# GpSimd's bias tables wait for VectorE's qk or low part, and five dot products move from mixer C to mixer B, in a two-layer hybrid encoder

## What is computed

```python
mod = jax.nn.silu(c) @ w_ada + b_ada                     # one row per token group
shift, scale, gate = jnp.split(mod, 3, axis=-1)
h = rms_norm(x, ln_g) * (1.0 + scale) + shift
qa, ka, va = ...   # mixer A: 4 heads, differential attention
qb, kb, vb = ...   # mixer B: 8 heads of 64, neighbourhood attention on a (rows x 64) grid
qc, kc, vc = ...   # mixer C: 12 heads of 128, three dilated windows
s = einsum(qr, kr) * scale + bias                        # B: bias from rpb_b, by relative position
s = jnp.where(col_ok, s, NEG); p = softmax(s)
merged = sum(sigmoid(g_i) * ((y_i * silu(z_i)) @ w_br[i]) for i in A, B, C)
x = x + gate * (merged @ w_out)
```

## Time and profile before

| | us |
|---|---|
| median of three runs | 2292.37 (2291.51 to 2294.75) |
| the profiled execution, device time | 2290.99 |
| its span, first to last instruction | 2289.2 |
| VectorE busy | 1716.5 (75%) |
| ScalarE busy | 1117.2 (49%) |
| GpSimd busy | 59.6 (3%), 103 instructions |

### The profile page before, as it was taken

One profiled execution on the slowest core, in us unless ns is written; L12 is line 12 of the kernel. 1 busy time (PEld: TensorE's weight loads), 2 busy tenths in 40 slices (PEclk: granted clock), 3 DMA queues, 4 the chain that ended last, 5 costly groups with the idle time before them and its releaser, 6 DMA issues.

```text
span 2289.2 us, 41733 instructions
## 1 busy us (share of the span) xinstructions
PE 2258.8 (99%) x15128; PEld 2124.0 (93%) x15128; DVE 1716.5 (75%) x4730; ACT 1117.2 (49%) x3063; POOL 59.6 (3%) x103
## 2 busy tenths in 40 slices
PE   7999999999999999999999999999999999999999
PEld 5888998999998999999888899899999989999998
DVE  7887789898886766677578867776898866676772
ACT  5676665434444434334357666654444353343340
POOL 0010110000000000000000102100000000000000
PEclk9999999999999999999999999999999999999999
DMA  7211123233111233321521211121121113332223
GB/s 288 82 56 63 64 66 108 102 112 107 58 50 46 85 109 121 102 102 65 163 98 36 86 61 45 58 85 61 65 80 50 48 53 104 109 120 91 89 95 117
DMA packets 78907, 200.28 MB, mean 87 GB/s; under 512 B 12272, under 2 KB 33392, under 8 KB 76912
## 3 DMA queue, kind: packets, MB, share of 16 engines
q1 hardware_dynamic: 57936, 155.09, 20.1%
q10 hardware_dynamic: 20768, 42.52, 5.4%
HBM read 176.59 MB, written 18.88 MB: 85 GB/s over the span
## 4 chain that ended last, share of the span: by engine, by line
PE 88%; DVE 6%; ACT 3%; issue 2%; DMA 1%; SPq 0%; ACTq 0%; DVEq 0%; POOL 0%
PE ps_proj L1127 53%; PE ps_score L1171 11%; PE ps_pt L1171 9%; PE ps_pt L1320 2%; PE ps_score L1304 2%; PE ps_pv L1356 2%; PE ps_score L1288 1%; PE ps_pv L1337 1%; PE ps_tr L1370 1%; PE ps_tr L1371 1%; PE ps_pv L1350 1%; PE ps_pt L1363 1%; PE ps_score L1294 1%; DVE gained L2159 1%; ACT w_hi L1510 1%
## 5 line engine op out<-in xcount | busy, mean ns | idle before, releaser
L1127 PE MATMUL ps_proj<-w_hi,act_hi 128*128 128x384 f32 x1800 | 623.7, 347 | 2.2 <-DVE act_lo L2339 1.4
L1127 PE MATMUL ps_proj<-w_hi,act_lo 128*128 128x384 f32 x1808 | 606.9, 336 | 0.0
L1127 PE MATMUL ps_proj<-w_lo,act_hi 128*128 128x384 f32 x1800 | 603.9, 335 | 0.0
L1127 PEld LDWEIGHTS ps_proj<-w_hi,act_hi 128*128 128x128 f32 x1800 | 338.3, 188 | 5.2 <-ACT act_hi L1590 2.5
L1127 PEld LDWEIGHTS ps_proj<-w_hi,act_lo 128*128 128x128 f32 x1808 | 339.5, 188 | 0.0
L1127 PEld LDWEIGHTS ps_proj<-w_lo,act_hi 128*128 128x128 f32 x1800 | 338.8, 188 | 0.0
L1687 ACT ACTIVATE square<-ps_proj 128x256 f32<-128x256 f32 x228 | 88.1, 387 | 226.2 <-PE ps_proj L1127 224.2
L2153 DVE TENSOR_REDUCE ssq<-square 128x2 f32<-128x256 f32 (+1 forms) x228 | 95.3, 418 | 133.4 <-ACT square L1687 132.6
L2527 DVE TENSOR_TENSOR w_lo<-w_raw,w_hi 128x1536 fp32r<-128x1536 f32 (+3 forms) x105 | 169.6, 1617 | 10.3 <-ACT w_hi L1510 9.5
L1510 ACT ACTIVATE w_hi<-w_raw 128x1536 fp32r<-128x1536 f32 (+2 forms) x104 | 144.2, 1387 | 41.9 <-DMA w_raw<-in_w 23.3
L2440 DVE TENSOR_TENSOR s_lo<-s_raw,s_hi 128x512 fp32r<-128x512 f32 x224 | 150.8, 685 | 9.3 <-ACT s_hi L1850 7.5
(11 more groups left out here) (264 smaller groups left out, 5127.8 us busy)
## 6 DMA issues: line engine op xcount, KB each, us to landing
w_raw<-in_w SPq DMA_DIRECT2D x80, 768.0 KB, 5.7
s_raw<-in_w_gate SPq DMA_DIRECT2D x96, 256.0 KB, 3.3
strip<-in_w_strip ACTq DMA_DIRECT2D x32, 512.0 KB, 3.6
w_raw<-in_w SPq DMA_DIRECT2D x24, 512.0 KB, 3.8
wb_raw<-in_w_branch SPq DMA_DIRECT2D x24, 512.0 KB, 3.6
first_ada<-in_w_first SPq DMA_DIRECT2D x8, 1024.0 KB, 12.9
w<-in_w_gate SPq DMA_DIRECT2D x32, 256.0 KB, 3.8
parked<-y_t ACTq DMA_DIRECT2D x4, 1536.0 KB, 5.1
```

The costliest lines, as they stand in the source:

```text
L1127: op = pe.matmul(out, sta[s](k), mov[m](k), start=(k == 0 and n == 0), stop=(k == chunks - 1 and n == 2))
```

## The change

In `dot_hosts` the six units of C's first group are no hosts any more. As the last free passes are taken, the five dot products that stood there go to the last five free ones before, which lie in mixer B. In `biases` every part waits in addition for what closes the list that its first wait belongs to: the low part if that list makes one, else the qk.

```diff
 SCORED, CROSSED, VALUED, TOPPED, COPIED, TAKEN = steps()
+TOP_AT = {a: n for n, some in TOPPED.items() for a in some}
...
-    free = [i for i in range(AT["q", l, "A", 1, 0, 2], AT["q", l, "C", 0, 0, 0] + MIX_FROM) if i not in LOW_IN and i not in busy]
+    free = [i for i in range(AT["q", l, "A", 1, 0, 2], AT["q", l, "C", 0, 0, 0] + MIX_FROM)
+            if i not in LOW_IN and i not in busy and UNITS[i][2:5] != ("C", 0, 0)]
...
+            def after_item(n):
+
+                if n in LOW_IN:
+                    pool.wait_ge(*w_lo_ready.at(LOW_IN[n]))
+                else:
+                    pool.wait_ge(*qk_ready.at(UNITS[n - 1]))
+
             def biases(l, h):
...
                         pool.wait_ge(*proj_ready.at(("q", l, "A", HEADS - 1, 0, part)))
+                        after_item(AT["q", l, "A", HEADS - 1, 0, part] + 1)
...
                         pool.wait_ge(*masked.at((l, "B", h - 1, last)))
+                        after_item(TOP_AT[l, "B", h - 1, last])
```

## The result

The changed kernel takes 2295.39 us (median of 22 runs, 2292.35 to 2300.01) against 2293.18 us for the kernel before, run beside it (22 runs, 2291.16 to 2298.25). The ratio is 1.0013, with an interval of 1.0007 to 1.0019: slower by 2.2 us by the medians and by 3.0 us by the ratio, where 2.6 us less were forecast. It is inside the 0.2% that the forecast called no change, but it has the other sign, and 2295.4 lies above the range's upper end, 2293.0. The profiled execution took 2294.16 us (span 2292.4 us), the one of before 2290.99 us (2289.2). The granted clock is 0.999.

What follows compares the result with a forecast made beforehand. PE, busy 99% of the span, was taken as the bound, so only its stalls could pay. -3.56 + 0.6 + 0.4 = -2.6 us took 2292.37 to 2289.8 us, range 2287.0 to 2293.0.

Steps and rivals of the forecast that it cites:

- (1): C's first group, first layer: five dot products leave lists 31, 32 and 35, ending PE stalls, -3.56 us.
- not the cause at 372.86: ScalarE's y_t wait, first layer: its 1.71 us stay for other reasons, only 1.85 us won, 2291.5 us; chance 0.08.
- (2): Lists 17 to 20 and 23: five dots arrive; list 24 late by 0 to 0.4 us, cost 0 by itself.
- the gate: SyncE's wait for list 24's last bias before head 3's tables and C's first weight; opening 1.08 us later.
- (3): Lists 15 to 30: GpSimd's biases wait for qk or low part; VectorE regains up to 1.28 us in each.
- a new GpSimd collision that delays ntop: Listed sign of a wrong forecast in the profile: GpSimd newly makes VectorE's ntop late; no place or size given.
- (4): SyncE's queue behind head 2's last bias: C's first weight later, costing PE 0.6 us first layer, 0.4 second.
- A straggler: C's first weight, second layer: 6.9 us from issue to ScalarE against 4.9, a delay other timing may remove.
- Low copy holds the bias back: After list 24's qk: VectorE's held-chunk copy delays the second bias, 0.61 us in both layers, 2291.0 us; chance 0.12.
- Weight in time: C's first weight, second layer: arrives without its delay, PE regains about 2.1 us, 2287.7 us; chance 0.18.
- Slower, by the gate: SyncE's queue: late weight, late list 24 and copy lock lose 4.3 us, +0.7, 2293.1 us; chance 0.06.

## Why the prediction was wrong

**(1) Right.** -3.56 us forecast for the five dots that leave, -3.58 measured, -3.59 with the dots alone. The rival in which they are not the cause at 372.86 is out, and no wait came in their place.

**(2) Right for its own places.** No PE wait in lists 17 to 23. The dot in list 23 alone makes list 24 start 0.42 us later, relative to its transposes (0.40 us behind them, 0.02 before them earlier), at the bound of 0.4. In the changed kernel it is 0.60 us, because there the scalings of list 23 take 1.62 us under GpSimd: the step counted on newton stalls that leave the list and not on what takes their place. That went into the gate.

**(3) The step that failed.** The prediction put it so: the biases start after the low part "beside the next list's first operations (ssq, gained and the masked scores, which read one SBUF operand at most)". That holds in mixer B. The first head's biases are made in mixer A, where the rotations stand ahead of the maxima. The step listed lists 15 to 30 and left 3 and 4 out: 1.24 + 1.20 = 2.44 us at 0. The text even names "a new GpSimd collision that delays ntop" among the signs of an error, and gives it no place and no price. By itself this term turns -2.6 into -0.2.

This cost stands in every profile: in the seven kernels without a new wait for the first head unit 5 takes 6.39 to 6.91 us in both layers, in the three that let it go by the low part 7.59 to 7.70 us.

The same part had a second error, which cost less. "VectorE gets back up to 1.28 us in each" counted the newton steps and not what runs after the qk. The scalings take 0.95 us of the 1.28 in list 24 and 1.0 us in list 29 (the sum behind the 1.28 makes 1.27). The reason given was the earlier trace rows, a pair "that began under GpSimd" in 0.64 us. GpSimd's instructions there run from 241.12 for 1.98 us, to 243.10, so of a pair from 242.87 on they could hold up 0.23 us at most; the row could not show what a full overlap costs.

**(4) Right mechanism, sizes too small.** The tables were to leave 1.08 to 1.45 us later and left 1.87 and 1.31 us later; of the first, 0.6 is the late list 24. At PE units 26 and 29 make +1.34 us in the first layer and +1.18 in the second, where 0.6 and 0.4 were taken (their sum, 2.52, lies just inside the bounds, 0 to 2.6). What the sum let go by: the weight's landing. "A straggler" was wrong. From SyncE's issue to ScalarE's start the fourteen such pieces of the seven profiles with this queue took 4.6 to 6.7 us in the first layer and 6.2 to 7.7 us in the second, so 4.9 in the first and 6.9 in the second are both ordinary. Also missing is the granted clock, which the step took as 1.00 throughout: in the second layer it fell to 0.50 behind the wait, and the cost came in unit 26 and not at the move, where the step looked for it. That the move ends behind ScalarE's high copies was right.

**The rivals.** *Low copy holds the bias back*: not in list 24, where the bias pair was over (298.62) before the copy began (298.70). It happens in list 28, where the group of four takes 2.62 and 2.27 us around the move's copies instead of 1.8. *Weight in time*: it never was. *Slower, by the gate*: the sign came out as this rival has it, +0.7 forecast for it. Its mechanism gave 2.5 us of the 3.56 from which it decides, and unit 5 the other 2.4. Together they are 5.0 us against 3.6.

**The sum again**, with what was measured: -3.58 + 1.34 + 1.18 + 2.44 = +1.4 us from the four terms. The medians differ by 2.2 us and the ratio gives 3.0 us (1.6 to 4.4), so 0.2 us to the lower end, 0.8 to the medians and 1.6 to the ratio are not accounted for by these terms. How much of it is landing times, the waits of the gate's part or the granted clock (0.995 and 0.997 as the mean of the two slowest executions of the changed kernel, 2300.01 and 2299.31 us, 0.999 in the profiled one), and how much something I didn't find, stays open.

## What to carry to other kernels

Two engines that exclude each other don't stop colliding when one is told to wait. Look up what the other runs at the new time, list by list in every stage that the code path serves, and prefer the place where the one that nobody waits for loses. And before a slow side engine is held back, read what its finish releases on a DMA queue: moving a weight ahead of a late table was worth about 4 us in the old kernel and about 8 us in the new one (from 1.0013 to 0.9976, two chips), for two moved lines.

## What I had not expected of the hardware

- The loser can be either engine, by as much: GpSimd's pair 1.6 to 3.24 us beside a low part, VectorE's rotation 0.43 to 1.10 us, a pair of scalings 0.62 to 1.57 us, GpSimd's four of 1.8 to 2.62 us beside the copies of the move.
- A scaling with one SBUF operand and scalars beside it waits for GpSimd as two-operand forms do.
- The same 768 KB load on the same queue, behind the same six tables, took 4.6 to 7.7 us from issue to use, in six of seven profiles longer in the second layer than in the first. With the weight first, the runs of a kernel also lie closer together (1.1 and 2.0 us from lowest to highest in 5 runs each, 2.8 and 4.0 us in 11, where 22 runs of the changed kernel spread over 7.7); fewer runs are part of that.
- A wait of PE can cost more than itself. Behind 1.90, 1.95 and 2.07 us in unit 26 the granted clock fell to 0.50 for 2 us and more and eight score products took up to 2.08 us instead of 1.14; behind 2.39, 2.44 and 2.88 us at the same place in other profiles it stayed at 1.00. What decides between them is not shown.
